# Giving up the unread TensorE products in front of the norms, the output tiles and the router of a two-layer decoder

## The reference, cut to what matters

```
for l in range(DEPTH):
    h = modulate(x, norm_mix_g[l], sh1, sc1)          # rmsnorm(x, g) * (1 + scale) + shift
    y = token_mixer(h, ...)                           # h @ w_in ... concat(...) @ w_out
    x = x + gt1[:, None, :] * y
    h = modulate(x, norm_ffn_g[l], sh2, sc2)
    if l % 2 == 0: f = swiglu(h, ffn_w_gate[j], ffn_w_up[j], ffn_w_down[j])
    else:          f = moe_ffn(h, router_w[j], router_b[j], ...)   # top_k(h @ router_w + router_b, 2)
    x = x + gt2[:, None, :] * f
return rmsnorm(x, final_norm_g)
```

## Time and profile before

| | |
|---|---|
| median of three runs | 1532.77 us |
| the profiled execution, its own time | 1530.87 us |
| its span, first to last instruction | 1528.6 us |
| mean granted TensorE clock | 0.984 |
| TensorE busy | 1454.6 us, 95% |
| VectorE busy | 1152.6 us, 75% |
| ScalarE busy | 787.3 us, 52% |

### The profile page before, as it was taken

The page is one execution under the profiler, slowest core; times in us unless marked ns, Lnnn a source line. Parts: engine busy times, 40 slices in busy tenths (PEclk is TensorE's granted clock), DMA queues, the critical chain, the costliest instruction groups (busy, mean ns, idle before and its releaser), DMA issues.

```text
span 1528.6 us, 24484 instructions
## 1 busy us (share of the span) xinstructions
PE 1454.6 (95%) x9962; PEld 1159.9 (76%) x9962; DVE 1152.6 (75%) x1429; ACT 787.3 (52%) x939; POOL 64.1 (4%) x50
## 2 busy tenths in 40 slices
PE   5999999999999999999999999899999999999993
PEld 3667877778888888877677777778888888888883
DVE  4979976876666655449488755789999999999984
ACT  3544347242222322235433565577777777777774
POOL 8200000000000000000000000300000000000001
PEclk9999999999999999999999999999999999999996
DMA  9463212646655664521111014699999999999975
GB/s 362 157 203 111 85 55 94 225 138 189 189 191 188 184 200 140 185 77 57 56 59 57 16 49 185 236 410 410 394 395 399 396 394 387 397 397 399 397 268 179
DMA packets 94607, 340.42 MB, mean 223 GB/s; under 512 B 10016, under 2 KB 14240, under 8 KB 91808
## 3 DMA queue, kind: packets, MB, share of 16 engines
q1 hardware_dynamic: 92048, 329.96, 59.1%
q0 software_dynamic: 2448, 8.91, 1.5%
HBM read 316.81 MB, written 22.02 MB: 222 GB/s over the span
## 4 chain that ended last, share of the span: by engine, by line
PE 84%; DVE 6%; DMA 4%; ACT 3%; issue 2%; POOL 1%; SPq 0%; POOLq 0%; DVEq 0%; ACTq 0%
PE ps L670 33%; PE ps L1298 10%; PE ps L1296 10%; PE ps L1297 10%; DVE scr L1820 2%; DMA scr<-in_ada 2%; PE ps L1025 1%; DVE scr L1817 1%; PE ps L1266 1%; PE ps L684 1%; PE ps L1258 1%; PE ps L996 1%; PE ps L1100 1%; PE ps L686 1%; PE ps L1101 1%
## 5 line engine op out<-in xcount | busy, mean ns | idle before, releaser
L1817 DVE TENSOR_TENSOR wlm<-rawm,hlo 128x2048 fp32r<-128x2048 f32 x120 | 274.6, 2289 | 15.9 <-ACT hlo L1406 14.9
L1337 ACT ACTIVATE whi<-raw 128x1024 fp32r<-128x1024 f32 (+1 forms) x112 | 123.7, 1104 | 279.6 <-PE ps L670 242.7
L1406 ACT ACTIVATE hlo<-rawm 128x2048 fp32r<-128x2048 f32 x120 | 230.2, 1918 | 71.4 <-PE ps L1298 70.0
L670 PE MATMUL ps<-hhi,whi 128*128 128x512 f32 x624 | 250.7, 402 | 1.8 <-DVE wlo L1827 1.2
L670 PE MATMUL ps<-hlo,whi 128*128 128x512 f32 x624 | 243.3, 390 | 0.0
L670 PE MATMUL ps<-hhi,wlo 128*128 128x512 f32 x624 | 243.3, 390 | 0.0
L1827 DVE TENSOR_TENSOR wlo<-raw,whi 128x1024 fp32r<-128x1024 f32 (+1 forms) x112 | 144.6, 1292 | 126.0 <-ACT whi L1337 123.5
L1297 PE MATMUL ps<-wlm,xgh 128*128 128x512 f32 x480 | 186.7, 389 | 0.0
L1817 DVE TENSOR_TENSOR wlm<-rawm,whm 128x2048 fp32r<-128x2048 f32 x60 | 137.4, 2291 | 30.7 <-ACT whm L1406 30.7
L670 PEld LDWEIGHTS ps<-hhi,whi 128*128 128x128 f32 x624 | 117.2, 188 | 38.1 <-issue 12.5
L1296 PE MATMUL ps<-hlo,xgh 128*128 128x512 f32 x360 | 141.7, 394 | 1.5 <-ACT xgh L1739 1.5
(11 more groups left out here) (338 smaller groups left out, 2443.7 us busy)
## 6 DMA issues: line engine op xcount, KB each, us to landing
rawm<-in_wm SPq DMA_DIRECT2D x360, 512.0 KB, 8.2
raw<-in_w SPq DMA_DIRECT2D x96, 512.0 KB, 3.6
adah<-in_ada SPq DMA_DIRECT2D x56, 512.0 KB, 4.5
scr<-in_ada SPq DMA_DIRECT2D x20, 1024.0 KB, 8.2
raw<-in_w SPq DMA_DIRECT2D x16, 704.0 KB, 5.1
xs<-scr SPq DMA_DIRECT2D x15, 512.0 KB, 5.8
ys<-yb SPq DMA_DIRECT2D x15, 512.0 KB, 9.2
xg<-xs SPq DMA_DIRECT2D x13, 512.0 KB, 7.4
```

The lines of the kernel that those rows point to most:

```text
L670: ins = pe.matmul(ps[:, b, :], a, r[:, k0 + k, :], start=(start and first and k == ks[0] and n == 0), stop=(stop and last and k == ks[-1] ...
L1337: act.activation(whi[:, slot, 0:width], raw[:, slot, 0:width], ACT.Copy).then_inc(sem("hi_ready"), 1)
L1406: act.activation(hi_pair(q), raw_pair(q), ACT.Copy).then_inc(sem("him_ready"), 1)
L1817: return dve.tensor_tensor(out, a, b, op)
```

## The change

The calls of busy in front of the first pair of tiles (4 in layer 0, 8 in layer 1), in front of the output tiles of layer 1 (2), in front of the first pair of the dense mixer (5) and in front of the router (6) go, 25 in all. Nothing else is touched, and the helper stays, without a caller.

```diff
@@ -964,7 +964,6 @@
                     args = (T_IN[layer] + t, t % 2, t % 2, hhi, hlo, 0)
                     if t == 0:
                         pe.wait_ge(sem("bank_free1"), U_IN[layer])
-                        busy(0, 8 if layer else 4)
                         first_pair(T_IN[layer], 16 * layer)
                         gates_of_tokens()
                     elif t == 1:
@@ -1133,8 +1132,6 @@
                 out_turned(3)
                 if layer == 0:
                     condition_rows(G_GATE)
-                else:
-                    busy(7, 2)
                 pe.wait_ge(sem("yhi_ready"), 6 * v - 2)
                 for w in range(2):
                     out_half(w, 2 * w, False)
@@ -1168,7 +1165,6 @@
                 if layer == 0:
                     for j in range(2):
                         pe.wait_ge(sem(f"bank_free{j}"), U_GU0)
-                    busy(0, 5)
                     first_pair(T_GU0, 8)
                     for i in range(1, FC):
                         for j in range(2):
@@ -1193,7 +1189,6 @@
 
                     iota = ps[:, 3, P:2 * P]
                     pe.matmul(iota, C("ones"), C("before"), start=True, stop=True)
-                    busy(1, 6)
                     for k in range(DC):
                         pe.wait_ge(sem("hs_ready"), k + 1)
                         j = 32 * (k % 4)
```

## The result

The change makes the kernel slower. Twenty runs of each: median 1542.38 us after (1530.92 to 1550.69), 1533.07 us before (1527.71 to 1538.31); the ratio is 1.0057, with an interval of 1.0042 to 1.0073, so +8.7 us (the two medians lie 9.3 us apart). The forecast was 1535.6, and the range ended at 1541.5.

A forecast was written before the change was run, and what follows sets the result against it. TensorE, busy 95% of the span, was taken to bound the kernel. Clock losses of 0.3 + 2.0 + 2.0 + 0 + 0.4 = +4.7 us, against nothing saved, took 1530.87 to 1535.6 us; range 1529 to 1541.5.

The forecast's parts named there:

- A: Four calls before layer 0's first pair: 0.58 us of the pair run at half speed, 0.3 us lost.
- None did: At the places of the removed products, no real TensorE product stood waiting behind them.
- B: Five calls before the dense mixer's first pair: a 4.15 us pause lowers the clock, 2.0 us lost, bounds 0 and 3.4.
- C: Eight calls before layer 1's first pair: a 4.15 us pause lowers the clock, 2.0 us lost, bounds 0 and 3.4.
- second rival: Pairs starting low keep the clock low; B and C two stretches each, A and E one: +10.2 us, 1541.1; chance 0.14.
- D: Two calls before layer 1's output tiles: pause of 0.94 us, no clock fall, 0 us, bounds 0 and 1.7.
- E: Six calls before the router: a 2.92 us pause, only the last chunk's tail late, 0.4 us, bounds 0 and 1.7.
- The first (no fall): Rival: the clock doesn't fall where forecast, or falls in pauses only; nothing changes, 1530.9 us; chance 0.13.
- The third: Rival: later work moves against the clock's steps and falls elsewhere might not recur; faster, 1527.1 us; chance 0.09.

The follow-up runs named there:

- third profile: The kernel before, unchanged, profiled a third time: 1537.72 us.
- e13: The kernel before with only A's four calls given up and the clears of xs issued early: 1531.62 us, ratio 0.9989 (0.9975 to 1.0003).
- second profile before: The kernel before, unchanged, profiled a second time: 1531.02 us.

## Why the prediction was wrong, step by step

**The step that failed is A, "0.3 us lost", together with what I took from "None did": as no real product stood behind those given up, I had removing them cost nothing but clock.** I costed removed instructions by TensorE's time alone. They are also part of the program's length: taking 16 records away moved every later border by 16 records, toward what looks like the losing side of a race that the kernel before already ran (4.3 us of waits in its third profile). That the loss at A is late fetches beside the clears is shown; how much of it comes of the shorter program, and how much would come by chance without it, stays open. A alone cost 5 to 7 us, and rows 4, on which I costed it, hold nothing of that. The clock's share, the 0.3 us that I did count, was even less: from its first to its last product A's pair took 13.42 us against 13.38. The rows that I left aside were the waits "issue" at L846, three of them with 2.3 us in all, in layer 1 of the trace before: nothing released them, and I took them for noise.

**B, 2.0 us, and C, 2.0 us: the mechanism was right, the size a little low.** In the seven profiles in which both pauses were idle, B's pair was 1.5 to 2.8 us longer and C's 1.8 to 2.5; B and C alone cost 5.2 us by the ratio, I had 4.0. B was low for 3.4 us in the cheap cases and 6.8 in the dear ones. The second rival's mechanism was at work here (a pair that begins low keeps the clock low), but at four fifths of its price: 2.7 us for 6.8 us of low clock and not 3.4, because part of the stretch lies in the pause itself. 5.44 of 6.83 us at C are busy.

**D, 0, and E, 0.4: right, as far as can be measured.** Together -0.01% with an interval of 0.2% on either side. L1195 took 5.68 us with a pause of 2.76 in front, and no low stretch lay on it, so the fall on which I costed E didn't come. After, the short products behind the router ran in a low stretch of 6.8 us and cost 1.0 us, and more than that was given back among the experts: the pause of 3.86 us before is one of 2.54 after, and no low stretch follows it.

**The rivals.** The first (no fall) is excluded by the clock at B and C. The second had the measured size, 1541.1, and not the cause, so its number is luck: it asked for low clock at A and E, and e13 shows A's clock to be free. The third named later work moving against the clock's steps; what moved was the program against its fetches. It was right that falls come and go: that of 997.5 is absent after, and those of 141.01 and 240.00 are new.

**The 7.0 us between A and B, taken apart.** Up to border 1473 nothing is lost (68.3 us from A's last product, before and after). From there to B's first L655 it is 182.2 to 182.5 us in the seven profiles with no low stretch on the way and at most 1.0 us of waits, 183.8 to 183.9 in the four with one low stretch of 3.4 us, and 189.3 after, with two. So one such stretch costs 1.5 us here, the two make 3.1 of the 7.0 us, and the 5.8 us of waits the other 4. The stretch at 141.01 is itself a price of a late fetch: all seven low stretches that begin between border 1473 and 185 us, in six profiles, begin within 2 us of a wait of 1.8 us or more, and the profiles without such a wait have none there. The one at 240.00 is not: the second profile before, without a late fetch, has one at 234.5.

The Trainium skill's rule ("TensorE: Matmul & The Clock Gate", section "HAM oscillation — how this bites in real kernels"), that a pause before a group of products makes the group start at half clock, agrees with B and C, where the two pairs began with 0.76 us records behind 3.99 us of idle time. It says nothing of the part at A.

## What to carry to other kernels

An instruction that does nothing may not be free to remove: its length places all later code against the borders of the fetched blocks. So look in the trace for waits of an engine that nothing released, at multiples of the same distance in its program, and for what large transfers are issued at that moment. Keep bulk transfers that have no hurry, such as clears, away from runs of very short products, which eat 256 records in 1.3 us: here it took 6 to 7 us off the kernel without A's products (1.0033 to 0.9989), and nothing off the kernel before. Filling a pause pays where wide products follow back to back (here two pauses of 4 us, 1.5 to 2.8 us each in the profiles), and not where the work behind it is paced by others.

## What the runs showed of the hardware that I had not expected

- TensorE's program is fetched in blocks of 16 KB, 256 records. In layer 0's inverse a fetch that began within 2.1 us of the last border cost less than 0.15 us where 4 us of work lay before the next border, and up to 2.0 us in front of records 2497 and 2753, where at times only some 2 us did; one that began 2.5 to 4.9 us behind it cost 0.4 to 2.9 us. Seven of the eleven waits of 1.8 us or more had a fall of the clock within 2 us.
- Transfers beside it make it late. With the clears moved, the packet began 1.0 to 1.6 us behind border 1473 in all four profiles; with the clears there it began 3.2 to 3.8 us behind in five of fifteen. Whether it is queued behind the two transfers of 512 KB was inferred from moving the clears, not seen: the trace has no time at which a fetch is requested.
- What decides at border 1473 is not known. With the clears there, a tile issued 0.02 to 0.08 us ahead of it let the fetch through in all eight profiles that had it, 0.10 and 0.11 us did not (one profile each), and 0.14 to 0.17 us did in two and did not in three. So the lead matters, by these few cases, but there is no single limit to it.
- A clock fall in front of a first pair lasts 3.4 or 6.8 us, and the same kernel shows either: B's was 6.8 us in two profiles of after and 3.4 in the third.
